# One step of a hybrid S5 / sparse-attention / MoE layer: the expert row table one tile sooner, gathers free of the stored base, the shared gate one tile ahead, the index projection in halves

## What is computed

```python
z = x @ w_in                                   # u, q, k, v, iq (512), ik (64), iw (8), gates
iq, ik = rope(iq), rope(ik)                    # index queries (8 heads x 64) and index keys (64)
ssm_out, h_re, h_im = s5_branch(u, h0, ...)    # a complex recurrence over the rows, in chunks
attn = dsa_attention(q, iq, iw, k, v, ik, ...) # index scores choose 256 keys per row
x = layer_norm(ALPHA*x + (g_ssm*ssm_out + g_attn*attn_out) @ w_out)          # x1
# MoE: 64 experts, 6 per row, rows sorted by expert into blocks of 128
routed = sum_over_blocks(swiglu(x1[rows of the block], w_exp_gu[e], w_exp_down[e]) * gate)
shared = swiglu(x1, w_sh_gu, w_sh_down)        # silu(a) * b, then down
y = layer_norm(ALPHA*x1 + routed + shared)
```

## Time and profile before

| what | value |
|---|---|
| runs (3) | 2154.71 us median, 2151.82 to 2157.92 |
| the profiled execution, its own time | 2152.48 us |
| its span in the trace | 2150.6 us |
| PE, DVE, ACT, POOL busy | 93%, 45%, 26%, 29% of the span |

### The profile page before, as it was taken

How to read it: one execution, slowest core, us unless ns; L and a number is a source line. 1 busy time by engine, 2 the same in 40 slices (tenths; PEclk the granted TensorE clock), 3 DMA queues, 4 the chain that set the end, 5 groups by cost and what they waited for, 6 DMA issues and landing times.

```text
span 2150.6 us, 23580 instructions
## 1 busy us (share of the span) xinstructions
PE 2000.3 (93%) x7670; PEld 1094.7 (51%) x7670; DVE 973.9 (45%) x2561; ACT 562.7 (26%) x1136; POOL 613.2 (29%) x792
## 2 busy tenths in 40 slices
PE   8999999999999999998999896999999999999980
PEld 6666645666655665566454463444444444444430
DVE  5373365999765542150355642333233332333326
ACT  2223553662566640030232000111111111111112
POOL 0031000010220001101222263455544555445534
PEclk9999999999999999999999998999999999999995
DMA  5040113110110011125211502999999999999995
GB/s 183 3 43 7 43 29 126 42 45 5 25 27 1 2 45 44 30 58 159 113 59 54 170 30 99 348 373 371 379 378 373 373 371 377 376 374 371 371 338 176
DMA packets 130469, 365.09 MB, mean 170 GB/s; under 512 B 34642, under 2 KB 82515, under 8 KB 112595
## 3 DMA queue, kind: packets, MB, share of 16 engines
q1 hardware_dynamic: 105250, 289.80, 36.0%
q0 software_dynamic: 23328, 72.90, 13.1%
q10 hardware_dynamic: 1808, 1.33, 0.2%
HBM read 310.82 MB, written 53.04 MB: 169 GB/s over the span
## 4 chain that ended last, share of the span: by engine, by line
PE 59%; DMA 19%; issue 7%; DVE 6%; POOL 6%; ACT 3%; POOLq 0%; SPq 0%; DVEq 0%; ACTq 0%
DMA arena<-x_d,tid 15%; PE psum L605 11%; PE psum L746 8%; PE psum L764 6%; PE psum L620 4%; PE psum L881 4%; PE psum L473 3%; POOL arena L1258 3%; ACT arena L1305 3%; PE psum L817 3%; PE psum L427 3%; PE psum L681 2%; PE psum L462 2%; DVE arena L2226 2%; PE psum L700 2%
## 5 line engine op out<-in xcount | busy, mean ns | idle before, releaser
L1305 ACT ACTIVATE arena<-psum 128x512 f32<-128x512 f32 (+7 forms) x641 | 285.1, 485 | 1171.9 <-PE psum L881 422.7
L881 PE MATMUL psum<-arena 128*128 128x512 f32 x1088 | 485.6, 599 | 47.6 <-DVE arena L2226 27.7
L881 PEld LDWEIGHTS psum<-arena 128*128 128x128 f32 x1088 | 202.0, 191 | 285.9 <-issue 285.7
L1258 POOL DMA_INDIRECT arena<-x_d,tid x276 | 265.6, 962 | 79.8 <-issue 70.4
L895 PE MATMUL psum<-arena 128*128 128x512 f32 x544 | 244.6, 592 | 0.5 <-ACT arena L1305 0.5
L605 PE MATMUL psum<-arena 128*128 128x384 f32 (+1 forms) x768 | 239.6, 471 | 0.1
L2232 DVE TENSOR_TENSOR arena<-arena,psum 128x256 f32<-128x256 f32 x68 | 28.7, 421 | 461.2 <-ACT arena L1305 434.5
L605 PEld LDWEIGHTS psum<-arena 128*128 128x128 f32 x768 | 144.2, 190 | 95.4 <-issue 11.4
L746 PE MATMUL psum<-arena 128*128 128x384 f32 (+1 forms) x576 | 179.1, 474 | 5.7 <-DMA arena<-in_w_attn_proj 5.6
L2226 DVE STREAM_TRANSPOSE arena<-arena 128x256 f32<-128x256 f32 x272 | 150.1, 609 | 65.7 <-DMA arena<-x_d,tid 64.7
L895 PEld LDWEIGHTS psum<-arena 128*128 128x128 f32 x544 | 103.3, 190 | 130.3 <-issue 129.6
(11 more groups left out here) (306 smaller groups left out, 2287.7 us busy)
## 6 DMA issues: line engine op xcount, KB each, us to landing
arena<-in_w_exp_gu SPq DMA_DIRECT2D x69, 2048.0 KB
arena<-in_w_exp_down SPq DMA_DIRECT2D x68, 1024.0 KB
arena<-in_w_in SPq DMA_DIRECT2D x24, 512.0 KB, 4.5
arena<-in_x_prompt SPq DMA_DIRECT2D x10, 512.0 KB, 4.2
arena<-x_d,tid POOLq DMA_INDIRECT x276
arena<-in_w_glu SPq DMA_DIRECT2D x16, 256.0 KB, 4.9
arena<-in_w_attn_proj SPq DMA_DIRECT2D x16, 256.0 KB, 4.6
arena<-in_w_out SPq DMA_DIRECT2D x1, 4096.0 KB, 12.9
```

The costliest lines, as they stand in the source:

```text
L881: last = mm(psum[:, 2, :], xgT[u][:, k, :], ewg[u][:, k, :], start=k == 0, stop=k == DK - 1)
L1258: pool.indirect_dma_start(xg[u][:, g, :], None, x1_d.rearrange("t (a f) -> (t a) f", a=4), bass.IndirectOffsetOnAxis(ap=tid[u][:, g:g + 1] ...
L1305: return act.activation(dst, src, fn, **kw)
```

## The change

Four edits. The index projection is cut into two halves of 292 columns, and the output store of a tile's index keys moves on ACT from behind the transposes to the start of the next tile's copies, where it waits for `zi_roped`. The shared expert's `shared_up` moves one tile ahead: tile 2's goes in front of `cnt`, and from then on `shared_up(i + 1)` stands where `shared_up(i)` stood; DVE's `gate_shared(0)` and the `spread` copies go in front of the block plan, `gate_shared(i)` for i from 1 on stays in iteration i. The slots are computed in two iterations instead of three, and the table work starts and ends one iteration sooner. POOL's wait for `base_stored` moves behind the first three gathers.

```diff
+HALF_I = 292
-        planned_in = lambda i: range(max(0, 11 * (i - 3)), max(0, min(NT * MK, 11 * (i - 2))))
+        planned_in = lambda i: range(max(0, 11 * (i - 2)), max(0, min(NT * MK, 11 * (i - 1))))
@@ z_index (PE)
-                for key, c0, n in (("iq", 0, 512), ("ik", 512, 72)):
+                for key, c0, n in (("iq", 0, HALF_I), ("ik", HALF_I, HALF_I)):
@@ second loop (PE)
+            shared_up(2)
             for i in range(NT + 1):
-                if 2 <= i < NT:
-                    shared_up(i)
+                if 3 <= i + 1 < NT and i > 0:
+                    shared_up(i + 1)
...
-                    if i == NT:
+                    if i == NT - 1:
                         pe.wait_ge(s("tab_ready"), 2)
@@ POOL
             pool.wait_ge(s("x1_stored"), 16 * NT)
-            pool.wait_ge(s("base_stored"), 16 * NT)
...
                 gather(m % 2)
             last_pair = pool.value_load(npair_i[0:1, 1:2], min_val=NE // 2 - 1, max_val=NBP // 2 - 1)
+            pool.wait_ge(s("base_stored"), 16 * NT)
@@ take_zi, take_turned (ACT)
+                if i >= 1:
+                    store_index_rows(i - 1)
...
-                f(z[:, 0:512], bank(("iq", i))[0:r, :])
+                f(z[:, 0:HALF_I], bank(("iq", i))[0:r, 0:HALF_I])
...
-                f(z[:, 512:576], bank(("ik", i))[0:r, 0:64])
-                f(iws[0:r, i, :], bank(("ik", i))[0:r, 64:72], scale=8 ** -0.5).then_inc(s("zi_ready"), 1)
+                f(z[:, HALF_I:576], bank(("ik", i))[0:r, 0:576 - HALF_I])
+                f(iws[0:r, i, :], bank(("ik", i))[0:r, 576 - HALF_I:HALF_I], scale=8 ** -0.5).then_inc(s("zi_ready"), 1)
+            def store_index_rows(i):
+                act.wait_ge(s("zi_roped"), i + 1)
+                act.dma_start(out["ik_p"][0, 0, tok(i), :] if i < NT - 1 else out["ik_s"][0, 0],
+                              zi[0:rows(i), i % 2, 512:576]).then_inc(s(f"ik_stored{i % 2}"), 16)
...
+                if i == NT - 1:
+                    store_index_rows(i)
                 take(("ikT", i), ikT[:, k0:k0 + r], bank(("ikT", i))[:, 0:r], "ikT_ready")
-                act.dma_start(out["ik_p"][0, 0, tok(i), :] if i < NT - 1 else out["ik_s"][0, 0],
-                              zi[0:r, i % 2, 512:576]).then_inc(s(f"ik_stored{i % 2}"), 16)
@@ DVE
+            for a in range(4):
+                last = dve.tensor_copy(spread[:, :, a, :], ident[:].rearrange("p (g i) -> p g i", i=32))
+            step(last)
+            gate_shared(0)
             await_bank(dve, "cnt")
...
-            for a in range(4):
-                last = dve.tensor_copy(spread[:, :, a, :], ident[:].rearrange("p (g i) -> p g i", i=32))
-            step(last)
             dve.wait_ge(s("x1_stored"), 16 * NT)
             for i in range(NT + 1):
-                if i < NT:
+                if 0 < i < NT:
                     gate_shared(i)
-                if i == NT - 1:
+                if i == NT - 2:
                     await_bank(dve, "tab")
...
-                if i < 3:
-                    for j in range(3 * i, 3 * i + 3):
+                if i < 2:
+                    for j in range(5 * i, min(NT, 5 * i + 5)):
                         slots(j)
-                if i == 2:
+                if i == 1:
                     block_and_place()
```

## The result

The changed kernel takes **2144.36 us** (median of 6 runs, 2142.77 to 2149.14); the kernel before took 2157.93 (median of its 6 runs, 2151.82 to 2160.11). The ratio is 0.9948 with a 95% interval of 0.9932 to 0.9963: faster, by 11 us (8 to 15). The profiled executions differ by 9.8 us: 2140.8 us of span against 2150.6. In what follows one of the nine runs of e2_halves, of 4185.25 us against 2143.68 to 2149.64 for the others, is left out of its ratio as a slow run.

The account below looks back on a forecast made before the run. PE, busy 93% of the span, paces the work from mix to routing; the expert-block loop has the DMA engines full. 9.9 us gained less 0.5 lost gives 9.4, so 2145.3 us against the median 2154.7; range 2141 to 2149.5.

Parts of the forecast that it names:

- Width: Index projection: two parts of 292 columns go by columns, saving about 0.85 us a tile of 128 rows.
- first sum: Index projection up to the mix, halves and moved store together: 9.9 us gained, and it lasts.
- The moved store: Index projection: tile 2's store leaves 0.8 us ahead of the m_op loads, removing a PE stall that lost 7.4 us.
- What comes next: Mix: PE then awaits m_op and the recurrence's end; what started at 179.54 starts 8.2 us sooner (7.5 to 8.9).
- It lasts: Between mix and routing: PE paces one string of work, so the 9.9 us gained before it arrives at its end.
- The bank waits: Second loop: PE waits 12.8 us at turn_hidden(1) in place of 4.0, and 2.7 us at shared_down(7), for reused banks.
- Second sum: Second loop to first expert product, bank waits against earlier gathers: 0.5 us lost, between 1 gained and 3 lost.
- the banks don't bind: Rival, second loop: PE waits only for gate_shared(1), then one-hot rows; 24 us gained there, 2131 in all; chance 0.08.
- The rhythm of the expert blocks: Rival, loop over 68 blocks: gathers behind weight loads delay each block, 0.25 us each costing 17 us, 2162; chance 0.06.
- The rival of the stuck store: Index projection: tile 2's store doesn't leave ahead of the m_op loads, PE's stall stays; 3.2 us gained, 2151.5; chance 0.18.

Follow-up runs that it names:

- e2_halves: Kernel before with only the index projection cut into halves of 292 columns, the store left behind the transposes: 2146.22 us (ratio 0.9963).
- e4_routing: Kernel before with only the routing and gather edits, index part as before: 2153.91 us (ratio 1.0004).
- e11_gathers: Kernel before with only POOL's wait for the stored base moved behind the first three gathers: 2146.24 us (ratio 0.9971).
- e6_base_wait: Changed kernel with POOL's wait for the stored base put back in front of the gathers: 2155.2 us (ratio 0.9998).
- e5_gates: Changed kernel with DVE's gate_shared one more tile ahead, gate_shared(1) and (2) in front of the slots: 2129.88 us (ratio 0.9892).
- e3_store: Kernel before with only the index keys' store moved, 512 and 72 columns kept: 2143.52 us (ratio 0.997).
- e9_slots_first: e7_cnt_first with three tiles' slots put in front of gate_shared(1) and (2): 2129.25 us (ratio 0.9893).
- e7_cnt_first: Changed kernel with DVE's gate_shared one more tile ahead and shared_up(2) behind cnt: 2133.61 us (ratio 0.9898).

## Why the prediction was right

The forecast was 2145.3 us, 9.4 us of gain; measured were 2144.36, and 9.8 in the profiled executions. The mechanisms were those named. That the sizes meet this closely is in part luck: at the first expert product 8.3 us were gained and not 9.4, and D, where no edit lies, happened to be 1.5 us shorter. Point by point:

- **Width.** 0.85 us a tile was forecast. From the start of tile 2 to the next tile it is 127.96 to 135.94, 7.98 us, against 8.72 before (129.78 to 138.50): 0.74. The timeline of PE before:

```profile
129.78 8.77 PE L473 MATMUL psum<-arena 128*128 128x512 f32 x32
138.39 0.27 PE L485 MATMUL psum<-ident,arena 128*128 128x128 f32 x1
138.50 8.77 PE L473 MATMUL psum<-arena 128*128 128x512 f32 x32
```

From the first product to the transpose behind it are 8.61 us. The 512-wide part takes 6.87 of them (the distance from 1246.87 to 1253.74 in the second loop), so 1.74 are left for the 72-wide part and not 1.84: it had a little less to give than its row suggested. Only four tiles (0, 1, 6 and 7) enter the first sum, so this is 0.4 us, less than A varies by.
- **The moved store.** Forecast: issued at 140.6, down near 142. It was issued at 141.14 and down 1.5 us later, with the loads of m_op issued from 141.26 (141.4 forecast). The margin was 0.12 us and not 0.8: the rotation took 4.52 us (136.58 to 141.10) where it had taken 3.99. That even this was enough is luck for the forecast. The margin was 0.10 to 0.12 us in all nine kernels with the moved store, and in all nine the store was down in 1.5.
- **What comes next.** m_op was awaited until 163.45 (163.8 forecast), the recurrence until 170.5 (170.5). Mix's second prompt part began at 170.53, 9.0 us sooner against 8.2 forecast: the granted clock was 1.00 from 160 to 180 us, so it did not fall in these pauses, and the better end of the range was taken. At the entry of the GLU stage 10.3 us were gained in this pair of executions, against 9.9; over the groups of three and of eight it is 8.3, and 9.2 from the start of the index projection on.
- **It lasts.** It did up to the attention; at the first shared_up it was 9.1 us (1177.3 against 1168.2).
- **The bank waits.** 12.8 and 2.7 us were forecast, 12.79 and 2.64 measured. shared_down(1) took 6.29 us where 5.9 was taken. First gather at 1304.22 (1304), first expert product at 1318.30 (1317).
- **Second sum.** 0.5 us lost was forecast. C shows 0.8 lost in the changed kernel and 0.5 gained in e4_routing, which has the same routing code: near nothing, and the sign is not shown. e11_gathers and e6_base_wait show how it is made: what the gathers gain, the rest takes back. So the rival "the banks don't bind", 24 us, which is how the edits look without the banks, failed in its first step. Its size was a little high as well: of its 24 us some 14 lay in this stretch, and with the banks out of the way e5_gates has a C 11.1 us under the one before, since DVE's slots and POOL's token rows come next.
- **The rhythm of the expert blocks** did not change: D is 822.5 to 824.5 in twelve of thirteen executions. The rival of the stuck store is what e2_halves shows: 3.7 us gained at the entry of the GLU stage by that rival, 2.2 in A and 3.5 from the start of the index projection on.
- **The Trainium skill's rules on DMA** (DMA: Bandwidth & Descriptors, section Queues, rings and completion order). That an engine takes turns between its queues did not make a store of 32 KB quick behind SP's backlog: 14.6 us in e2_halves, 12.4 in the changed kernel. Its other rule, that a completion is written only after the earlier writes of that engine across its queues, agrees with the stores seen, above all the one issued at 161.32, down at 165.7 with the last load down at 165.5; no run tells it apart from other causes.

The forecast of the median was 0.9 us off, less than the measurement can tell, and that it is so close is luck: the median of before, from which it was counted, moved from 2154.71 to 2157.93 as runs were added. The two medians of 6 runs differ by 13.6 us and the ratio says 11, so the size of the gain is known to a few microseconds only.

## What to carry to other kernels

Where buffers are handed out in turn, moving one producer ahead changes whose buffer every later claim gets: write the claims down in order and look up which reader each one waits for, and where that reader stands in its engine's queue. A wait taken away in one place (the gathers here) can pay for one that was added in another, and the total then hides both: run each edit alone. And a small store that somebody waits for belongs in front of a burst of loads, not behind it.

## What I had not expected

**The attention of the running stream does not always get the full clock.** B varies from 907.7 to 918.5 us between kernels that are the same there, and it goes with the granted TensorE clock from 900 to 960 us. The windows view, first e3_store, then e9_slots_first; the columns are the window, its length, busy us of PE, PEld, DVE, ACT and POOL with counts, the granted clock, the DMA share and GB/s:

```profile
920.00:960.00 40.00, 39.57 (x398) 26.29 (x395) 21.41 (x73) 12.31 (x16) 0.86 (x1) 1.00 0.34 108
```

```profile
920.00:960.00 40.00, 39.58 (x376) 26.26 (x374) 20.78 (x71) 10.60 (x14) 0.00 (x0) 0.71 0.16 41
```

PE is busy for the same 39.6 us, but the clock is 1.00 in one (2.4 GHz throughout) and 0.71 in the other, a mixture of its two levels (1.2 and 2.4 GHz). From 900 to 960 us the mean clock was 1.00 in the three executions with a B under 908 (e2_halves, e3_store, e11_gathers), 0.91 in before, after, e4_routing, e5_gates, e6_base_wait and e7_cnt_first (910 to 913), and 0.83 or 0.77 in the four with a B above 915. The stage consists of short products and transposes; what decides between the levels there was not tried. It is seen in whole runs as well: of 50 runs of the kernel before, taken in three sets, those with a clock of 0.966 took 2162 to 2164 us and those with 0.975 took 2145 to 2146, and the medians of the three sets lie between 2152.14 and 2158.07. For a gain of 10 us this is a noise of the same size, and it is the reason to compare stretches and not spans.

**POOL's token rows** hold PE up in e5_gates and e7_cnt_first, between one-hot products. In e5_gates POOL begins them at 1217.29, 2.0 us before PE's first one-hot product; in e9_slots_first at 1220.10, 5.2 us before, and there PE does not wait.
